# Inverting the chunk matrices of a delta-rule recurrence as 64x64 pairs in the two halves of TensorE, instead of as 128x128 block-diagonal matrices

## The reference, cut to what matters

```python
def step(S, inp):
    w_t, k_t, v_t, kk_t, a_t = inp[:5]
    sa = jnp.einsum('bhvk,bhk->bhv', S, kk_t)
    S = (S * w_t[:, :, None, :]
         - sa[..., None] * (kk_t * a_t)[:, :, None, :]
         + v_t[..., None] * k_t[:, :, None, :])
    y = jnp.einsum('bhvk,bhk->bhv', S, inp[5]) if emit else None
    return S, y
```

## Time and profile before

| | |
|---|---|
| median of 3 runs (lowest to highest) | 6765.76 us (6764.06 to 6787.76) |
| profiled execution: time, span | 6769.53 us, 6767.7 us |
| TensorE matmul busy | 3779.0 us (56%) |
| VectorE busy | 3974.9 us (59%) |
| ScalarE busy | 1153.8 us (17%) |
| GpSimd busy | 1834.1 us (27%) |
| mean granted TensorE clock | 0.76 of full speed |

### The profile page before, as it was taken

How to read it: one execution, slowest core, us unless ns; L and a number is a source line. 1 busy time by engine, 2 the same in 40 slices (tenths; PEclk the granted TensorE clock), 3 DMA queues, 4 the chain that set the end, 5 groups by cost and what they waited for, 6 DMA issues and landing times. The chain is left out here.

```text
span 6767.7 us, 72149 instructions
## 1 busy us (share of the span) xinstructions
PE 3779.0 (56%) x24704; PEld 3191.6 (47%) x24704; DVE 3974.9 (59%) x7160; ACT 1153.8 (17%) x2534; POOL 1834.1 (27%) x1562
## 2 busy tenths in 40 slices
PE   8777887377777503277650068788800000354888
PEld 1566776266667402166640057677600000353777
DVE  0355663656888685778879833565277789433110
ACT  0112331011333000023320011333100000111110
POOL 0000000032443373024457710000018877300000
PEclk9888998699888756588765589798855555676899
DMA  8221002166665696156679943000329999510333
GB/s 315 98 90 47 1 1 72 53 255 230 199 211 164 242 347 242 48 179 211 217 244 366 352 143 118 7 1 7 100 81 323 332 346 362 195 37 14 108 120 115
DMA packets 295491, 1115.41 MB, mean 165 GB/s; under 512 B 33312, under 2 KB 38704, under 8 KB 289968
## 3 DMA queue, kind: packets, MB, share of 16 engines
q0 software_dynamic: 221184, 805.40, 33.9%
q1 hardware_dynamic: 74032, 306.33, 13.0%
HBM read 1110.55 MB, written 1.05 MB: 164 GB/s over the span
## 5 line engine op out<-in xcount | busy, mean ns | idle before, releaser
L153 PE MATMUL psum<-h,weight_ring 128*128 128x256 f32 x5440 | 1218.4, 388 | 144.9 <-PEq L79 133.5
L153 PEld LDWEIGHTS psum<-h,weight_ring 128*128 128x128 f32 x5440 | 1059.6, 195 | 303.7 <-issue 139.4
L1268 POOL DMA_INDIRECT ring<-in_peer_u,expert x496 | 596.6, 1203 | 1749.7 <-SPq L79 856.2
L1485 DVE SCALAR_TENSOR_TENSOR tok<-ring,act,tok 128x1024 f32<-128x1024 f32 x688 | 884.0, 1285 | 108.5 <-DMA ring<-in_peer_v,expert_group 66.4
L1521 PE MATMUL psum<-constants,tok 128*128 128x128 f32 x48 | 10.6, 413 | 1581.6 <-PEq L79 1581.6
L1437 POOL DMA_INDIRECT ring<-in_peer_v,expert_group x688 | 783.0, 1138 | 228.4 <-issue 215.8
L1521 PEld LDWEIGHTS psum<-constants,tok 128*128 128x128 f32 x48 | 9.6, 223 | 1582.3 <-issue 1582.3
L1248 DVE CUSTOM_DVE_ANT_0 ring<-ring,tok 128x1024 f32<-128x1024 f32 x496 | 596.5, 1223 | 157.9 <-DMA ring<-in_peer_u,expert 142.4
L1437 POOL DMA_INDIRECT ring<-in_peer_u,expert_group x272 | 345.3, 1270 | 857.3 <-DVE expert_group L1473 779.0
L1480 DVE CUSTOM_DVE_ANT_0 ring<-ring,tok 128x1024 f32<-128x1024 f32 x272 | 330.8, 1226 | 89.5 <-DMA ring<-in_peer_u,expert_group 86.6
L401 PE MATMUL psum<-squares,constants 128*128 128x256 f32 x246 | 85.9, 523 | 218.7 <-ACT squares L383 218.7
(11 more groups left out here) (478 smaller groups left out, 7154.4 us busy)
## 6 DMA issues: line engine op xcount, KB each, us to landing
weight_ring<-in_w_in SPq DMA_DIRECT2D x228, 512.0 KB
ada_ring<-in_ada_w SPq DMA_DIRECT2D x24, 2048.0 KB
weight_ring<-in_w_q SPq DMA_DIRECT2D x48, 512.0 KB
weight_ring<-in_w_out SPq DMA_DIRECT2D x32, 512.0 KB
weight_ring<-in_w_gate SPq DMA_DIRECT2D x32, 512.0 KB
weight_ring<-in_w_mlp_in SPq DMA_DIRECT2D x32, 512.0 KB
weight_ring<-in_w_mlp_out SPq DMA_DIRECT2D x8, 2048.0 KB
weight_ring<-in_w_oB SPq DMA_DIRECT2D x24, 512.0 KB
```

Source lines behind the costliest of these rows:

```text
L153: mm = pe.matmul(k.bank(slot, tokens), ring[:, slot, j * P:j * P + P], rhs(j), start=(j == 0), stop=(j == w.kt - 1))
L1268: pool.indirect_dma_start(job.ring[:, r % HOSTED, :], None, job.tables[kind], bass.IndirectOffsetOnAxis(ap=job.eidx[:, number:number + 1], ...
L1485: dve.scalar_tensor_tensor(job.tok[:, tile, :], r.ring[:, j, :], r.act8[:, part, j:j + 1], job.tok[:, tile, :], ALU.mult, ALU.add).then_in ...
```

## The change

A new function `invert_pairs` takes the place of `invert_unit_lower` in the recurrence. All its matrices (Ld, LdT, NT, E1, E2, E3, X, TT) are half as wide: partition half hh holds head hh's 64x64 matrix, and 64 columns instead of 128 hold a pair. A product of one group is 8 matmuls of 64x64x64, two for each pair, one in each half of the array. Both halves of a group write the same PSUM bank, in their own partitions, 256 columns wide. All copies, sums and masks are one instruction over 128 partitions and 256 columns. The product that transposes X is a matmul by the identity.

LdT and NT now come from the "lower" product too: it is made in both orders (32 matmuls of 64x64 instead of 16), group i in bank 4 + i, and it signals after each group. G is masked two at a time after the first two products, and the first of them waits for all Gram matrices. `low_rank` waits for G. X is made after the copies of the first product. R is accumulated for both heads in one bank and copied by one ScalarE instruction; U is made by four 64x64 matmuls instead of two 128x128. E3 has a buffer of its own. GpSimd clears only W. Five new masks are added to the table of constants.

```diff
-def invert_unit_lower(k, block, groups, Ld, LdT, NT, temps, TT, ahead=None, banks=(0, 1, 2, 3), ready=None, between=None, banks_read=None):
+def invert_unit_lower(k, block, groups, Ld, LdT, NT, temps, TT):
...
+def invert_pairs(k, block, unit):
...
+    banks = (6, 7, 4, 5)
+
+    def product(q, g):
+        return k.bank(banks[(2 * q + g) % 4], 256).rearrange("p (h c) -> p h c", h=4)
+
+    copied = {(-1, g): (k.vec_step.sem, unit.ready[g]) for g in range(2)}
+
+    on_scalar = range(0 if k.job is not None else 1, 2)
...
+                dve.wait_ge(k.multiplied.sem, k.multiplied.at(2 * q + g + 1))
+                if added is None:
+                    ins = dve.tensor_copy(out[:, g], product(q, g))
+                else:
+                    ins = dve.tensor_tensor(out[:, g], product(q, g), added[:, g], ALU.add)
+                ins.then_inc(k.vec_step.up(), 1)
+                copied[q, g] = k.vec_step.sem, k.vec_step.count
+            unit.between(q, dve)
+            use_rows(k, dve, 1)
...
+                sem, value = copied[q - 1, g]
+                pe.wait_ge(sem, value)
...
+                for n in range(4):
+                    for hh in range(2):
+                        h = half(hh)
+                        rhs = k.ident[h, h] if right is None else right[h, g, n, :]
+                        mm = pe.matmul(product(q, g)[h, n, :], left[h, g, n, :], rhs, start=True, stop=True)
+                mm.then_inc(k.multiplied.up(), 1)
+            if q == 9 and unit.following is not None:
+
+                pe.wait_ge(k.vec_step.sem, unit.marks["G"])
+                unit.following.low_rank(pe)
...
             for i in range(2):
-                for hh in range(2):
-                    h = half(hh)
-                    dve.tensor_tensor(b.Ld[h, i, :, h], k.bank(4 + hh)[h, 256 * i:256 * i + 256].rearrange("p (n t) -> p n t", n=4),
-                                      masked(back[ways[i]][h, h], 4), ALU.mult).then_inc(k.vec_step.up(), 1)
+
+                dve.wait_ge(k.multiplied.sem, k.multiplied.at(lower + i + 1))
+                for turn, (out, mask) in enumerate(((b.Ld, back), (b.LdT, near))):
+                    dve.tensor_tensor(out[:, i], pairs(i, turn), masked(mask[ways[i]], 4), ALU.mult).then_inc(k.vec_step.up(), 1)
+                marks["ready", i] = k.vec_step.count
...
-                        c, at = 2 * i + n, 256 * i + (2 * n + j) * 64
+                        c, at = 2 * i + n, (2 * n + j) * 64
                         for hh in range(2):
                             h = half(hh)
-                            mm = pe.matmul(k.bank(4 + hh)[h, at:at + 64], KR[h, 0, j, 64 * c:64 * c + 64], b.C[h, j, c, hh, :], start=True, stop=True)
-            mm.then_inc(k.multiplied.up(), 1)
+                            kt, nb = KR[h, 0, j, 64 * c:64 * c + 64], b.C[h, j, c, hh, :]
+                            pe.matmul(k.bank(4 + i)[h, at:at + 64], kt, nb, start=True, stop=True)
+                            mm = pe.matmul(k.bank(4 + i)[h, 256 + at:320 + at], nb, kt, start=True, stop=True)
+                mm.then_inc(k.multiplied.up(), 1)
...
+        def between(q, dve):
+
+            if q == 0:
+                for i in range(2):
+
+                    dve.wait_ge(k.vec_step.sem, marks["ready", i])
+                    dve.tensor_tensor(b.X[:, i], b.Ld[:, i], masked(k.pair_ident, 4), ALU.add).then_inc(k.vec_step.up(), 1)
+                    marks["X", i] = k.vec_step.count
+            if q == 0:
+
+                dve.wait_ge(k.multiplied.sem, grams_made)
+            if q < 2:
+                i = q
+                for hh in range(2):
+                    dve.tensor_tensor(b.G[:, hh, i, :, 0:cols], k.bank(2 * i + hh).rearrange("p (n t) -> p n t", n=4)[:, :, 0:cols],
+                                      masked(k.gram_mask[ways[i]][hh][:, 0:cols], 4), ALU.mult).then_inc(k.vec_step.up(), 1)
                 marks["G"] = k.vec_step.count
...
-                    for hh in range(2):
-                        h = half(hh)
-                        ins = act.activation(R[h, i], k.bank(2 * i + hh)[h, 0:P].rearrange("p (j v) -> p j v", j=2), ACT.Copy)
-                    ins.then_inc(k.act_step.up(), 1)
+                    act.activation(R[:, i], k.bank(2 * i)[:, 0:P].rearrange("p (j v) -> p j v", j=2), ACT.Copy).then_inc(k.act_step.up(), 1)
...
                     for j in range(2):
-                        at = 64 * j
-                        mm = pe.matmul(k.bank(2 * i + 1)[:, at:at + 64], b.TT[:, i, 2 * (c % 2) + j, :], R[:, i, j], start=True, stop=True)
+                        for hh in range(2):
+                            h, at = half(hh), 64 * j
+                            mm = pe.matmul(k.bank(2 * i + 1)[h, at:at + 64], b.TT[h, i, 2 * (c % 2) + j, :], R[h, i, j], start=True, stop=True)
                     mm.then_inc(k.multiplied.up(), 1)
```

More of the change, by code:

```diff
@@ L468, in _ @@
                 copied[q, g] = k.vec_step.sem, k.vec_step.count
-            if between is not None:
-                between(q, dve)
+    @block.scalar
+    def _(act):
+        act.wait_ge(k.act_step.sem, k.act_step.mark)
+        for q, (_, _, added, out) in enumerate(steps):
+            for g in on_scalar:
+                if added is None:
+                    act.wait_ge(k.multiplied.sem, k.multiplied.at(groups * q + g + 1))
+                    act.activation(grp(out, g), product(q, g), ACT.Copy).then_inc(k.act_step.up(), 1)
+                    copied[q, g] = k.act_step.sem, k.act_step.count
@@ new lines, in _ @@
+    @block.tensor
+    def _(pe):
+        for q, (left, right, _, _) in enumerate(steps):
+            for g in range(groups):
+                sem, value = copied[q - 1, g]
+                pe.wait_ge(sem, value)
+                if right is X and q == 3:
+                    pe.wait_ge(k.vec_step.sem, started[g])
+                for h in range(4):
+                    out = product(q, g)[:, h, :]
+                    if right is None:
+                        mm = pe.transpose(out, grp(left, g)[:, h, :], ident)
+                    else:
+                        mm = pe.matmul(out, grp(left, g)[:, h, :], grp(right, g)[:, h, :], start=True, stop=True)
+                mm.then_inc(k.multiplied.up(), 1)
@@ new lines, in invert_pairs, with half, _ @@
+def invert_pairs(k, block, unit):
+    Ld, LdT, NT, E1, E2, E3, X, TT = unit.Ld, unit.LdT, unit.NT, unit.E1, unit.E2, unit.E3, unit.X, unit.TT
+    def half(hh):
+        return slice(64 * hh, 64 * hh + 64)
+    steps = [
+        (LdT, Ld, None, E1),
+        (Ld, LdT, None, E2),
+        (E1, E2, None, E3),
+        (E2, X, X, X),
+        (E3, X, X, X),
+        (X, None, None, TT),
+        (NT, X, None, E1),
+        (X, NT, None, E2),
+        (E2, E1, None, E3),
+        (E1, E2, None, Ld),
+        (Ld, E3, None, LdT),
+        (E1, TT, TT, TT),
+        (E3, TT, TT, TT),
+        (LdT, TT, TT, TT),
+    ]
+    banks = (6, 7, 4, 5)
[3 more added lines that the diff above has]
+    on_scalar = range(0 if k.job is not None else 1, 2)
+    @block.vector
+    def _(dve):
+        for q, (_, _, added, out) in enumerate(steps):
+            for g in range(2):
+                if g in on_scalar and added is None:
+                    continue
+                dve.wait_ge(k.multiplied.sem, k.multiplied.at(2 * q + g + 1))
+                if added is None:
+                    ins = dve.tensor_copy(out[:, g], product(q, g))
+                else:
+                    ins = dve.tensor_tensor(out[:, g], product(q, g), added[:, g], ALU.add)
+                ins.then_inc(k.vec_step.up(), 1)
+                copied[q, g] = k.vec_step.sem, k.vec_step.count
+            unit.between(q, dve)
@@ L648, in _ @@
             def _(pool):
-                for t in (b.Ld, b.LdT, b.NT, b.W):
-                    pool.memset(t[:], 0.0).then_inc(k.pool_step.up(), 1)
+                pool.memset(b.W[:], 0.0).then_inc(k.pool_step.up(), 1)
                 marks["cleared"] = k.pool_step.count
```

92 lines of the change are left out of this document (35 added, 57 removed).

## The result

The changed kernel takes 6448.95 us (median of 4 runs, 6431.19 to 6474.93) against 6765.16 us for the kernel before (4 runs on the same chip, 6764.06 to 6787.76). The ratio is 0.9528, with the interval 0.9489 to 0.9567: faster by 4.7%, 316 us. The forecast was 6526 with a range from 6455 to 6680. The sign and the mechanism came out as written; the gain, forecast at 240 us, was a third larger. The profiled execution took 6445.06 us, its span 6443.3.

What follows compares the result with a forecast made beforehand. Neither TensorE nor VectorE fills the span; plain units were taken as set by the product-evacuation loop, hosted ones by VectorE. Gains of 152 and 88 us, 240 in total, gave 6529.5 profiled and a 6526 us median, range 6455 to 6680.

Steps and rivals of the forecast that it cites:

- the plain unit's sum: Plain unit: gains 3.0 + 4.9 + 2.6 + 0.5 less 1.5 make 9.5 us, 152 us over 16 units.
- Clock ... I subtract 1.5 us: Plain unit: TensorE's pauses in products 1 to 3 lose the clock for two stretches, 1.5 us off the gain.
- Scan ... Gain 0.5: Plain unit's scan: R's single copy frees ScalarE, though VectorE is later anyway in the first step; gain 0.5 us.
- Products 1 to 3: Plain inversion's start, with X and G masks among the copies: 8.6 us falls to 5.6, gain 3.0.
- Products 4 to 10, and 11 to 14: Plain inversion: seven latency-bound steps of 1.2 us, 8.4 in all, gain 4.9; the last four products gain 2.6.
- Before the inversion: Plain unit: doubled "lower" but no wait for Gram matrices; first product after 4.8 us against 4.9, nothing gained.
- Hosted units: Units hosting expert rows, paced by VectorE: 5.8 + 2 - 2 - 0.3 = 5.5 us each, 88 us over 16.
- VectorE over 90% busy: Sign expected in a hosted unit, along with DMA waits up by about 2 us.
- mostly goes: Hosted inversion: the part of VectorE's 7.5 idle us that waits for TensorE mostly disappears, taken as 2 us.
- 1 and 4, a falling clock: Clock falls in half the inversion: 6630 us, chance 0.16; or stays at 1.2 GHz from "lower" to scan: 6859, 0.06.
- 2, one bank makes the halves take turns: Matmul halves sharing a bank run in succession, 0.10 us each, a step of 1.64 us: 6622 us, chance 0.11.
- 3, the gathers: Gathers at 2.43 us per row set the hosted units, which keep their length: 6614 us, chance 0.05.

Runs made afterwards that it cites:

- The last run: Changed kernel with G masks and sigmoids moved later and six hosted rows instead of four, plus idle matmuls in the hosted units: 6282.00 us, ratio 0.9305.
- The ring of six: Changed kernel with a ring of six hosted rows instead of four: 6448.96 us, ratio 0.9538 to the kernel before.

## Why the prediction was wrong in size, and what in it was right

**Failed step: the plain unit's sum, in two of its terms, "Clock ... I subtract 1.5 us" and "Scan ... Gain 0.5".** The mechanism was right and these sizes were off: the plain units gained 81 us more than forecast, and that is what carried the time below the range. Means over seven units of the first call, us:

| | before | after | gained | forecast |
|---|---|---|---|---|
| before the inversion | 5.4 | 5.7 | -0.3 | 0 |
| inversion | 32.0 | 20.7 | 11.4 | 10.5, less 1.5 for the clock |
| scan | 13.6 | 11.0 | 2.6 | 0.5 |
| rest of the unit | 5.2 | 4.6 | 0.5 | 0 |
| unit | 56.2 | 42.0 | 14.2 | 9.5 |

Here the inversion ends with TensorE's last matmul. The sum behind it, which the forecast counts with the inversion, is in the rest; it gained 0.25 us.

- *Clock.* Every plain inversion ran at 1.00, though TensorE pauses in each step. The prediction subtracted 1.5 us; measured, it should have added 0.3, because the kernel before loses its clock in two of these seven inversions (32.9 us at 0.95 beside 31.7 at 1.00) and the new one in none. That is 1.8 us of the 4.7 per unit. In the mask stretch of products 1 to 3 TensorE works for 3.5 of 4.9 us, more than the 2.9 of 5.6 that the caution rested on.
- *Scan.* 2.6 us, not 0.5: about 1.1 for the copy itself, and about 1.4 because the scans mostly keep their clock (1.00 in 14 of 16, before in 2). The copy was forecast as hidden in the first chunk step; it was on the path in both. That the clock goes when TensorE pauses in the scan is shown by the two runs with idle matmuls. Why it goes less often in the changed kernel is not: its pause before S is 0.95 us and was 1.01, and the kernel before with the scan's edits still lost it in 9 of 16 scans with pauses of 0.95 us. The clock part was in view: the earlier trace rows show 0.90 over a scan, and that reading was used as a risk to the new inversion, never as time that the scan itself was losing. 2.1 us of the 4.7.
- *Products 1 to 3.* 4.94 us where 5.6 were counted; 0.7 more gained.
- *Products 4 to 10, and 11 to 14.* 8.32 and 6.30 us, forecast 8.4 and 6.3. The loop of 0.48 + 0.23 + 0.42 + 0.05 measured 1.21 us for a step.
- *Before the inversion.* 5.0 us at full clock, forecast 4.8; where the clock is down, 7.85 instead of 6.9, since "lower" has twice the matmuls. That costs the 0.3 us of the table.

Over 16 units: 233 us, forecast 152.

**Hosted units.** 6.4 us each (64.2 to 57.8), forecast 5.5; 102 us for 88. VectorE's instructions sum to 58.7 us before and 52.9 after: the 5.8 us of the forecast. Its waits for TensorE fell by 0.8 us, not 2, and those for rows rose by 0.9, not 2: both too large, and they cancel. The sign "VectorE over 90% busy" did not show: in the window above it is busy for 83%. What "mostly goes" hid is that a wait for TensorE of 4 us per unit stayed, at a clock of 0.75 in these calls. The last run shows, in a kernel with 8.0 us of it, that most of such a wait goes when the clock is held.

**Outside the calls** nothing was forecast, and 11 us were lost. The stretch between the first two calls was 649.6 us before and 657.9 after, 655 to 664 in the other versions built on the changed kernel. It was 652 in the kernel with the scan's edits alone, but 663 in the kernel before with idle matmuls. Outside all four calls together, the profiles of the kernel before and its three variants have 4825 to 4859 us, and those of the changed kernel and its variants 4823 to 4877. The 11 us lie within that scatter, so no cost of the change is shown there.

**The rivals.** 1 and 4, a falling clock: the opposite happened in plain units. In the hosted units the clock did fall, from 0.95 to 0.91 in the mean of their inversions (0.88 in the window) and from 0.69 to 0.58 in their scans, without their losing what they gained. 2, one bank makes the halves take turns: refuted by 0.058 us per matmul; the gains listed under that rival sum to 6.0 us in the inversion, which would then stand at 25.7 us and not 20.7. (Less 1.3 us for "lower" they give 4.7 us a unit, where the prediction has 4.5.) The rule of the Trainium skill (TensorEngine Tiling (Array Packing), Gotcha 1: PSUM Pressure) that row tiles cannot use one bank at the same time does not hold for this pair of tiles, which differ in both their rows and their columns; the measurement decides. 3, the gathers: in the last version a hosted unit uses 27 rows in 53.3 us, 1.97 us for a row where this rival's limit was 2.43.

## What to carry to other kernels

A product in small matmuls that alternate between the two halves of the array costs half as much, and then the loop from a product through its evacuation to the next sets the pace: price it by that loop, and look for what VectorE or ScalarE does ahead of the copy that closes it. Read the clock of every stretch of the kernel before, not only of the one that changes, and count a clock below 1.00 as time to be won: an edit that shortens another engine's link in the chain can shorten TensorE's pause (here from 0.25 and 1.22 us to 0.95), and that can be worth more than the link. Where a pause can't be removed, a few idle matmuls in it are an experiment of three lines, and here they were worth 0.6% of the kernel before, and 1.2% in the last version, where they lie in the hosted units.

## What the runs showed of the hardware

- **Two halves in one bank.** Two 64x64x64 float32 matmuls, one in each half of the array, that write different partitions of one bank overlap as fully as in two banks: 0.058 us each at clock 1.00 (the earlier trace rows give 0.06). Without alternation they take 0.09.
- **The clock can fall for a pause of about a microsecond that recurs.** With R's two copies, and pauses of 0.25 and 1.22 us in each chunk step, the plain scans of the changed kernel ran at 0.62 to 0.85 and took 13.3 to 14.8 us in 13 of 16 units, and 11.8 at 1.00 in 3. With eight idle matmuls in the longer pause all 16 ran at 1.00 and took 11.8. The pause alone does not decide: at 0.95 us the clock fell in 2 of 16 scans of the changed kernel, in 5 of 16 when it was run again, and in 9 of 16 of the kernel before with the scan's edits. The Trainium skill (TensorE: Matmul & The Clock Gate, A second HAM failure mode) tells of a clock that swings when the engine idles briefly between groups; the scans agree. The plain inversions, whose pauses are about 0.2 us a step and once 1.02 us (at product 3), do not swing at all.
- **Pairs of matmuls in the two halves can hold the full clock.** All 16 plain inversions, 64x64 pairs but for the eight matmuls of `low_rank`, ran at 1.00, and idle pairs were enough to bring a hosted inversion from 0.87 to 1.00.
- **Relieving one wait can bring out another.** The ring of six took 3 us of row waits from a hosted unit, and waits for TensorE grew by 5.7 us, with the inversions' clock at 0.85 after 0.91 in the mean and at 0.70 in one. Why the clock fell just then was not separated from the order in which the rows come.
